# Attention 0 with one group of lead: the next group's maxima and exponentials ahead of this group's scaling and copies, and a third buffer of probabilities

## The reference

```python
s_loc = einsum(q, k_latent) * ATTN_SCALE          # window mask (A heads) or bias and mask (B heads)
s_ctx = einsum(q, k_context) * ATTN_SCALE
p = softmax(concatenate([s_loc, s_ctx, sink]))    # the sink for A heads only
o = einsum(p_loc, v_latent) + einsum(p_ctx, v_context)
# context queries: softmax over the 256 context keys alone (with the sink for A heads)
yx = concatenate([oa, ob]) @ w_out
```

## Time and profile before

| | us |
|---|---|
| median of 3 runs | 1885.76 |
| lowest, highest | 1885.32, 1886.61 |
| profiled execution | 1890.0 |
| its span, first to last instruction | 1887.8 |
| granted TensorE clock, mean of the span | 0.966 |

### The profile page before, as it was taken

The page is one execution under the profiler, slowest core; times in us unless marked ns, Lnnn a source line. Parts: engine busy times, 40 slices in busy tenths (PEclk is TensorE's granted clock), DMA queues, the critical chain, the costliest instruction groups (busy, mean ns, idle before and its releaser), DMA issues.

```text
span 1887.8 us, 24162 instructions
## 1 busy us (share of the span) xinstructions
PE 1754.6 (93%) x9428; PEld 1216.9 (64%) x9428; DVE 786.9 (42%) x1239; ACT 663.3 (35%) x954; POOL 35.9 (2%) x52
## 2 busy tenths in 40 slices
PE   5999999899999999999878999999899999999897
PEld 3885457688888777876666566555565566555553
DVE  2334553733323254653753433333342433433344
ACT  2324554422222233424733333333333333333241
POOL 1200000000000000000020000000000000000000
PEclk8999989899999999899988999999999999999999
DMA  9725752223323545321018999999989999999986
GB/s 330 189 97 181 246 176 68 67 89 99 124 79 100 202 178 178 111 90 45 1 32 371 421 417 421 421 421 402 421 358 400 382 420 420 421 421 383 414 356 257
DMA packets 111471, 481.81 MB, mean 255 GB/s; under 512 B 8154, under 2 KB 46216, under 8 KB 62208
## 3 DMA queue, kind: packets, MB, share of 16 engines
q1 hardware_dynamic: 108768, 472.66, 64.0%
q0 software_dynamic: 2592, 7.62, 1.8%
HBM read 477.38 MB, written 2.87 MB: 254 GB/s over the span
## 4 chain that ended last, share of the span: by engine, by line
PE 73%; DVE 10%; DMA 8%; ACT 6%; issue 3%; SPq 0%; DVEq 0%; ACTq 0%
PE PS L792 18%; PE PS L793 17%; PE PS L794 17%; DMA RAWB<-in_w_exp_up 5%; PE PS L1326 4%; PE PS L1399 3%; PE PS L814 2%; DMA RAWA<-in_w_exp_down 2%; ACT BH L1855 2%; PE PS L1012 2%; PE PS L1273 1%; DVE RAWAL L2560 1%; ACT S L1609 1%; PE PS L1022 1%; DMA RAW<-in_w_mod 1%
## 5 line engine op out<-in xcount | busy, mean ns | idle before, releaser
L1981 DVE TENSOR_TENSOR WL<-RAW,WH 128x2048 fp32r<-128x2048 f32 (+1 forms) x61 | 137.6, 2256 | 310.7 <-ACT WH L1526 310.6
L792 PE MATMUL PS<-HH,WH 128*128 128x512 f32 (+1 forms) x584 | 226.2, 387 | 8.2 <-DVE HL L2068 4.6
L793 PE MATMUL PS<-HL,WH 128*128 128x512 f32 (+1 forms) x584 | 223.0, 382 | 0.0
L794 PE MATMUL PS<-HH,WL 128*128 128x512 f32 (+1 forms) x584 | 222.8, 382 | 0.0
L1526 ACT ACTIVATE WH<-RAW 128x2048 fp32r<-128x2048 f32 (+1 forms) x61 | 115.1, 1887 | 261.1 <-PE PS L794 229.9
L792 PE MATMUL PS<-BH,HE 128*128 128x512 f32 x448 | 181.6, 405 | 19.3 <-DVE RAWAL L2560 12.9
L2560 DVE TENSOR_TENSOR RAWBL<-RAWB,BH 128x2048 fp32r<-128x2048 f32 x42 | 96.3, 2292 | 208.6 <-ACT BH L1855 208.6
L794 PE MATMUL PS<-BH,LE 128*128 128x512 f32 x448 | 176.1, 393 | 0.0
L1855 ACT ACTIVATE BH<-RAWB 128x2048 fp32r<-128x2048 f32 x42 | 80.4, 1914 | 228.4 <-DMA RAWB<-in_w_exp_up 136.1
L2560 DVE TENSOR_TENSOR RAWAL<-RAWA,BH 128x2048 fp32r<-128x2048 f32 x41 | 93.9, 2289 | 147.9 <-ACT BH L1855 147.7
L792 PEld LDWEIGHTS PS<-BH,HE 128*128 128x128 f32 x448 | 84.5, 189 | 84.0 <-issue 30.2
(11 more groups left out here) (329 smaller groups left out, 2746.9 us busy)
## 6 DMA issues: line engine op xcount, KB each, us to landing
RAWA<-in_w_exp_up SPq DMA_DIRECT2D x112, 1024.0 KB, 10.2
RAWB<-in_w_exp_up SPq DMA_DIRECT2D x112, 1024.0 KB, 10.0
RAWA<-in_w_exp_down SPq DMA_DIRECT2D x56, 1024.0 KB, 9.9
RAWB<-in_w_exp_down SPq DMA_DIRECT2D x56, 1024.0 KB, 9.7
RAW<-in_w_mod SPq DMA_DIRECT2D x48, 1024.0 KB, 5.4
RAW<-in_w_ffn_up SPq DMA_DIRECT2D x22, 1024.0 KB, 5.1
RAW<-in_w_in_c SPq DMA_DIRECT2D x12, 1024.0 KB, 5.2
RAW<-in_w_ffn_down SPq DMA_DIRECT2D x10, 1024.0 KB, 6.7
```

The lines of the kernel that those rows point to most:

```text
L792: mm(ps, ah, bh, start=start, stop=False)
L793: mm(ps, ah, bl, start=False, stop=False)
L794: return mm(ps, al, bh, start=False, stop=stop)
L1981: v.tensor_tensor(WL[:, c % 2, 0:n], raw("weight", c)[:, 0:n], WH[:, c % 2, 0:n].bitcast(F32), ALU.subtract).then_inc(s_lo, 1)
```

## The change

A third buffer SX joins the two of S, and groups use them in turn (`probs0`). TensorE makes the scores of groups 0 and 1 ahead of the loop, and in iteration i those of i+2: units 0 and 1 at its head, units 2 and 3 after the four turns. VectorE does front i+1, then normalise i, mod_columns, block_lo i-1. ScalarE does sinks and exps of i+1, then the four copies of i, mod_row_out, block_hi i.

```diff
+        SX = sb("SX", [P, 4, 512], F32, 80 * K)
...
+        def probs0(gi):
+
+            return SX[:, :, :] if gi % 3 == 2 else S[:, gi % 3, :, :]
...
                 scores(0, *gs[0], range(4))
+                scores(1, *gs[1], range(4))
                 for i, (b, g) in enumerate(gs):
-                    if i + 1 < len(gs):
-                        scores(i + 1, *gs[i + 1], (0, 1))
+                    if i + 2 < len(gs):
+                        scores(i + 2, *gs[i + 2], (0, 1))
...
                     if i < MOD_ATT:
                         mod_half(MOD_PRE + i, 0, 7)
-                    if i + 1 < len(gs):
-                        scores(i + 1, *gs[i + 1], (2, 3))
                     turn(i, b, g, 0)
                     turn(i, b, g, 1)
                     if i < MOD_ATT:
                         mod_half(MOD_PRE + i, 1, 7)
                     turn(i, b, g, 2)
                     turn(i, b, g, 3)
+                    if i + 2 < len(gs):
+                        scores(i + 2, *gs[i + 2], (2, 3))
                     weigh(i, b, g, 0)
                     weigh(i, b, g, 1)
...
                 for i, (b, g) in enumerate(gs):
                     nk = n_keys(0, b)
+                    if i + 1 < len(gs):
+                        sinks(i + 1, gs[i + 1][1])
+                        for j in range(4):
+                            exps(i + 1, gs[i + 1][0], j)
                     for j in range(4):
                         n = 4 * i + j
                         act.wait_ge(s_ptp, n + 1)
                         if i >= 1 and j % 2 == 0:
                             act.wait_ge(s_ops, 2 * (i - 1) + j // 2 + 1)
                         fn(PT0[:, j, 0:nk], PS[:, 2 + n % 2, 0:nk], ACT.Copy).then_inc(s_ptc, 1)
-                        if j == 1 and i < MOD_ATT:
-                            mod_row_out(MOD_PRE + i, 7)
-                    if i + 1 < len(gs):
-                        sinks(i + 1, gs[i + 1][1])
-                        for j in range(4):
-                            exps(i + 1, gs[i + 1][0], j)
+                    if i < MOD_ATT:
+                        mod_row_out(MOD_PRE + i, 7)
                     block_hi(i)
...
-                        if j == 0 and gi >= 2:
-                            dve.wait_ge(s_ptp, pts_before(gi - 1))
+                        if j == 0 and gi >= 3:
+                            dve.wait_ge(s_ptp, pts_before(gi - 2))
...
                 front(0, *gs[0])
-                normalise(0)
...
                 for i, (b, g) in enumerate(gs):
                     if i + 1 < len(gs):
                         front(i + 1, *gs[i + 1])
-                    if i >= 1:
-                        block_lo(i - 1)
+                    normalise(i)
                     if 1 <= i <= MOD_ATT:
                         n = MOD_PRE + i - 1
                         mod_columns(n, n + 1, 6)
-                    if i + 1 < len(gs):
-                        normalise(i + 1)
+                    if i >= 1:
+                        block_lo(i - 1)
                 block_lo(NG0 - 1)
```

More of the change, by code:

```diff
@@ L1022, in turn @@
                         last = nc.tensor.transpose(PS[:, 2 + n % 2, kt * P:(kt + 1) * P],
-                                                   S[:, i % 2, j, kt * P:(kt + 1) * P], ident)
+                                                   probs0(i)[:, j, kt * P:(kt + 1) * P], ident)
                     last.then_inc(s_ptp, 1)
@@ L1608, in exps @@
                         act.wait_ge(s_nm, gi + 1)
-                    fn(S[:, gi % 2, j, 0:nk], S[:, gi % 2, j, 0:nk], ACT.Exp, bias=NM(gi)[:, j:j + 1],
+                    fn(probs0(gi)[:, j, 0:nk], probs0(gi)[:, j, 0:nk], ACT.Exp, bias=NM(gi)[:, j:j + 1],
                        accum_out=SU(gi)[:, j:j + 1]).then_inc(s_exp, 1)
@@ L2108, in front @@
                                 BIAS[:, b - 2, 4 * (g - 2) + j, :]
-                            v.tensor_tensor_reduce(out=S[:, gi % 2, j, CTX:TOK], in0=PS[:, u % 2, CTX:TOK], in1=add,
+                            v.tensor_tensor_reduce(out=probs0(gi)[:, j, CTX:TOK], in0=PS[:, u % 2, CTX:TOK], in1=add,
                                                    scale=SCALE, scalar=-3e38, op0=ALU.add, op1=ALU.max,
                                                    accum_out=mx[:, 2 * j:2 * j + 1])
-                            v.tensor_tensor_reduce(out=S[:, gi % 2, j, 0:CTX], in0=PS[:, u % 2, 0:CTX],
+                            v.tensor_tensor_reduce(out=probs0(gi)[:, j, 0:CTX], in0=PS[:, u % 2, 0:CTX],
                                                    in1=ZERO[:, 0:CTX], scale=SCALE, scalar=-3e38, op0=ALU.add,
@@ L2116, in front @@
                         else:
-                            v.tensor_tensor_reduce(out=S[:, gi % 2, j, 0:nk], in0=PS[:, u % 2, 0:nk],
+                            v.tensor_tensor_reduce(out=probs0(gi)[:, j, 0:nk], in0=PS[:, u % 2, 0:nk],
                                                    in1=ZERO[:, 0:nk], scale=SCALE, scalar=-3e38, op0=ALU.add,
@@ L2143, in normalise @@
                         for j in (2 * pair, 2 * pair + 1):
-                            v.tensor_scalar(S[:, i % 2, j, 0:nk], S[:, i % 2, j, 0:nk], RI(i)[:, j:j + 1], None,
+                            v.tensor_scalar(probs0(i)[:, j, 0:nk], probs0(i)[:, j, 0:nk], RI(i)[:, j:j + 1], None,
                                             ALU.mult).then_inc(s_nrm, 1)
```

## The result

The changed kernel took 1867.49 us (median of 4 runs, 1864.07 to 1869.64), the kernel before 1886.18 in the same comparison: a ratio of 0.9895, 95% interval [0.9873, 0.9917]. So it is faster, by some 20 us. The profiled execution took 1864.07, the lowest of its four runs, for a span of 1862.1.

What follows compares the result with a forecast made beforehand. TensorE bounds it, 93% busy, losing time to waits and low clock. Stage: 166 + 46.5 + 45.2 + 18.9 = 276.6 against 305.80, 29.2 less 3, gain 26; 1890.0 becomes 1864.0, less 4.2 gives 1859.8; range 1853 to 1872.

Steps and rivals of the forecast that it cites:

- that cover: Iterations 8 to 12: second pair of scores starts 2.96 before weighing ends; VectorE's negated maxima done 0.1 to 0.5 after.
- Its other cover: Iterations 8 to 12: ScalarE can start turn copies at 3.2, before they are ready at 3.7; holds by 0.5.
- The uncovered exponentials: Iterations 13 to 15: without halves or scores as cover, copies wait behind ScalarE's exponentials; sum 18.9.
- 3 given back: Iteration 14: TensorE's wait from 1.0 to 3.9 may lower the clock; 3 us deducted, bounds 0 and 6.
- its own mechanism: Attention 0: TensorE is the bound at 2.4 GHz; 1859.8, between 1854 and 1865, chance 0.66.
- The 4.2: Whole kernel, last step: median of runs taken as 4.2 below the profiled one, turning 1864.0 into 1859.8.
- B: Iterations 1 to 13: clock as low as before, about 24 us of it, costing 8 us; 1868, chance 0.14.
- E: Most of attention 0 at low clock, so slower; 1912 if all of it is low, chance 0.05.
- C: Iterations 1 to 12: TensorE has room, ScalarE's ring sets the pace; 11 more gained, 1849, chance 0.03.
- the Trainium skill's rule on occupancy: TensorE in attention 0: matmul occupancy is no good measure of its limit; weight-load share is, so pieces would shrink.
- D: Iterations 1 to 12: a new wait replaces the old one; 13 of the 26 left, 1873, chance 0.08.
- F: Attention 0: no change, as VectorE's queue still ties scores to scaling through the buffers; chance 0.04.

Runs made afterwards that it cites:

- the loaded kernel before: Kernel before with one extra 128 x 512 copy each on ScalarE and VectorE in iterations 0 to 12, against the kernel before: 1901.32 us, ratio 1.0082.
- filling the wait: Identity transposes in TensorE's wait from iteration 8, against the kernel before: 1884.90 us (0.9997); with extra ScalarE and VectorE copies too, 1894.46 (1.0046).

## Why the prediction was right, point by point

*Iterations 8 to 12.* Forecast 5 x 9.04 = 45.2, measured 45.78. Four took 9.04; iteration 8 took 9.64, because its first scores waited for VectorE to empty the banks of a 512-key group, with a 256-key weighing of only 1.02 between. The prediction worked out that cover for 512 keys alone, where weighing is 1.90. Its other cover, ScalarE free 0.5 before the first turned unit, was 0.21.

*Iterations 1 to 7.* Forecast 46.5, measured 47.37: 6.44 for each of 1 to 5 (6.4 forecast), 7.29 and 7.88 for 6 and 7 (7.2 each), the second by the same missed wait: from the start of its first pair of scores to the next piece it is 1.65 in place of 1.06.

*Iterations 13 to 15.* 7.94 (7.9 forecast), 8.39 (6.75 plus the clock) and 4.45 (4.2). The uncovered exponentials were the right place: the second turns start 3.94 into iteration 14 (3.9). TensorE does not wait in one piece for them, as forecast, but 0.65 before the first turns and 2.13 before the second. The clock was low behind that in both profiles of the changed kernel (0.80) and iteration 14 was 1.6 longer than forecast, against 3 given back. That it would fall was not certain: a wait of 2.81 in the same place did not bring it down with two buffers, nor did one of 1.89 in iteration 14 of the first profile of before.

*Iteration 0.* It ended at 164.35 and 165.90 in two executions; the bounds were 164.6 and 167.5, and 166 was taken. The waits for maxima in it are 0.61 or less after the scores' first one of 0.67, in place of 2.88. What separates the two executions is the granted clock, 1.00 and 0.75.

*The sum.* The stage was to end at 276.6, with 3 given back for the clock at 279.6 (bounds 276.6 and 282.6); it ended at 278.3 and 279.9. The profiled execution was to take 1864.0 and took 1864.07. That exactness is luck, as errors cancel. In the first profile iteration 0 ended 1.65 sooner than taken, and that makes up for the 0.9 and 0.6 of the missed waits in iterations 1 to 12. The clock took 1.4 less than given back, and the rest of the span is 1.8 longer after (1582.9 against 1581.1), within what that rest scatters.

*What was mis-sized.* It is the median: 1859.8 was forecast, 1867.49 and 1864.87 were measured. The whole forecast, 1853 to 1872, holds both, but the first lies above the 1854 to 1865 that the prediction gave its own mechanism. The step is the last one, "The median of the runs is 4.2 below the profiled one, so 1859.8". The 4.2 was not a fixed offset between a profiled execution and the median: the changed kernel's profiled executions were 3.4 below its first median and 0.8 above its second. The likely reason is that the profiled execution of before had more low clock in attention 0 than usual (stage end 306.74, and 301.66 in the second). The change removes just that, so it must not be subtracted again. By this reading the gain of 26 belongs to one execution, and against the median the same stage is worth some 20. It rests on two profiles of the kernel before; the second was 5.9 above its own median, with the excess outside this stage.

*The rivals.* B (clock low in iterations 1 to 13) named the value nearest to the first median, 1868, but not the cause: the clock was 1.00 in all of them, twice. Its price was too low: a third for each us was read from scores (2.76 for 1.81), while in iteration 12 before turns took 1.90 for 1.02 and a half 1.86 for 1.00, about half of each us; E has the same fault. What it was said to have for it, equal waits that ended differently, is not in the profile the prediction read, but it is in the second one of before. C (TensorE has room): halves took 1.00 and turns 1.02 as before; by the Trainium skill's rule on occupancy (Perfetto Trace Analysis, Identifying the Most-Contended Engine), as the prediction read it, they would have shrunk. D, the block's copy as a new wait: it is there, 1.83 on ScalarE, and delays nothing in 1 to 12. A wait of the same kind, turns for copies behind the exponentials, is there in 13 (0.90) and 14 (2.13). E (the clock stays low) did not come; the fullest iterations had the full clock. F (no change) would have been the case without the third buffer (1.0003).

## What to carry to other kernels

When an engine that should be the bound waits once per iteration inside a ring (a closed chain of engines that wait for each other), give it its work one group further ahead, with one more buffer, and let one of the other engines lead too. Leading on TensorE alone cost 5%, two buffers gave nothing. Then lay out the iterations at the ends, where no other work covers the wait: there the order that is harmless in the middle costs 3 us in the profiles, though the times can't tell it. And before a sum is made against one profiled execution, ask how that execution stands to the median within the very stage that changes; an offset that lives there is part of the gain, not beside it.

## What the hardware showed that I had not expected

The granted clock makes small waits dear. Half a microsecond more per iteration on ScalarE cost the kernel before 15 to 18 us, as each of iterations 8 to 12 took 13.6 to 14.6 at a granted clock of 0.75 to 0.77; at 1.00 and without the added copy two of them take 10.2. A piece at the low clock is up to 1.9 times as long: a half of a modulation row 1.86 in place of 1.00.

Which wait brings the clock down was not found. The same wait of 0.70 in the same instruction was followed by the low clock in one execution of the kernel before and by the high one in the other, and the same in iteration 12. Waits of 0.93 to 1.72 in iterations 8 to 12 of the loaded kernel before were all followed by it. Waits of 0.98 after the turns, with two buffers, never were, nor was one of 2.81. In iteration 0 of the second execution of before, the half ahead of the long wait already took 1.93, so there the fall came first and the wait of 1.99 after it:

```profile
156.66 1.93 PE L814 MATMUL PS<-RAW,ST 128*32 128x512 f32 x8
160.58 1.56 PE L1012 MATMUL PS<-KTT,QT 64*128 64x256 f32 x4 [1.99 <-DVE SM L2117]
```

So the prediction's reading, that the clock fell after a wait of 0.70 and stayed high after one of 0.41, holds for the execution that it read and is no rule. No run varied what stands around a wait alone, and filling the wait did not settle it. What does hold is that with three buffers and at least one other engine in the lead, iterations 1 to 12 had a granted clock of 1.00 in all seven profiles; TensorE waited once in them, 0.58 with VectorE's order back.

The clock also makes runs scatter: the kernel before spread from 1879.9 to 1891.9 in 12 runs, the changed one from 1862.4 to 1865.7 in 6.
